# Forty of the sixty-four tile transposes of a decoder layer moved from TensorE to the DMA queue of SyncE

## The chip, the cores and the metric

The kernel runs on the 8 cores of one Trainium2 chip. Each core takes one of the 8 sequences of the batch and computes the whole layer for it; the cores exchange nothing. The metric is device time in microseconds of the slowest core: 1814.36 us as the median of 3 runs of the kernel before (1813.77 to 1814.71). The profile is that of the slowest core, core 4, in one execution.

A core has five engines that run side by side, each through its own list of instructions in order: TensorE (PE) multiplies, ScalarE (ACT) and VectorE (DVE) do the element-wise work and empty the PSUM banks that TensorE writes, GpSimd (POOL) does some element-wise work and issues the loads of the weights, SyncE (SP) issues the other transfers. They wait for one another through semaphores.

## The reference

The layer works on x, 2048 rows of 1024 columns in float32 per core:

```
x = x + 0.5 * swiglu(rmsnorm(x, ffn1_norm), w1, w3, w2)          # first FFN, 2816 wide
h = rmsnorm(x, mix_norm)
u = h @ w_in                                                      # q, k, v, gate, lru x, lru gate
y_ret = (silu(g_ret) * groupnorm(retention(rotary(q), rotary(k), v))) @ w_ret_o
y_lru = (rg_lru(conv(x_lru)) * gelu(g_lru)) @ w_lru_o
g = sigmoid(h @ w_branch_gate + b_branch_gate)
x = x + (g[:, :D] * y_ret + g[:, D:] * y_lru) @ w_out
x = x + softmax(q(rmsnorm(x, xattn_norm)) k(rmsnorm(mem)).T / 16) v @ w_xo   # 256 memory rows, 4 heads
x = x + 0.5 * swiglu(rmsnorm(x, ffn2_norm), ...)                  # second FFN
out = rmsnorm(x, final_norm)
```

So x is normalised five times, and four of the five results (all but the last) are the input of a matrix product.

## The kernel before, in words

x lies in SBUF as 16 tiles X of 128 rows x 1024 columns (tile tt holds rows 128 tt to 128 tt + 127). Four tiles make a row block of 512 rows, called tb. A matmul needs the normalised x with its columns on the partitions, so each tile is turned: hT holds, for each row block, eight pieces of 128 columns by 512 rows in bf16.

`norm_T` does this for one tile. `rstd_of` sums the squares on ScalarE (JUNK), scales on VectorE (stat) and takes the power -0.5 on GpSimd; VectorE writes the normalised tile in bf16 to HB, one of four buffers used in turn (line 936); then the tile is turned. With a PSUM bank given, eight matmuls with the identity write it to that bank (line 948), and ScalarE and VectorE in turn copy the bank into hT (lines 749 and 956). With `bk` None, a transposing transfer on SyncE's queue goes from HB straight to hT:

```
        if bk is None:
            P.add("sp", lambda e: e.dma_start_transpose(out=dst_ap, in_=hb.ap),
                  reads=hb.hs, writes=dst_hs, cost=400, dma=128 * D * 4)
            return
```

`norm_x(tt, row, bk)` calls it for tile tt, four times per tile: at the start (before the first FFN), in `post1` (after the first FFN, for the mixers), in `tail` (after the mixers' output product, for attention) and after attention (for the second FFN). In the three later places a number decides which of the two ways a tile goes:

```
norm_x(tt, mixrow[0], None if tt < TR1 else bkT)     # post1
norm_x(tt, row, None if tt >= TR2 else bkT)          # tail
norm_x(tt, rowf, None if tt < TR3 else bkT)          # after attention
```

In the kernel before, no tile goes by DMA. The handles that track who reads and writes hT cover two tiles each (`hhs(tb, j // 2)`), so the second tile of a pair is a later writer of the same handles as the first.

The stages follow one another: the first FFN in weight groups of 6, 6, 5 and 5 pieces, with the preparation of the memory and of tables in its gaps; the mixers (16 steps of the recurrent unit, 16 blocks of retention, 16 pieces of the gate product GW, whose results go to HBM); `tail`; attention (`scores`, then `outp` per tile); the second FFN; the last norm and the stores. During the mixers x gives up its place: `park` stores each tile to HBM after the first FFN, and `tail` loads it back. `ret_load` loads the weights RW of the retention, `load` in `lru_stages` those of the recurrent unit, LW.

The order of each engine's instructions is not written out by hand. The program first records all operations with their dependencies, an assumed cost and, for transfers, a byte count. `schedule` then plays them through: each engine takes the operation that can start first, and of several the one with the longest path behind it; transfers go by the latest start that a former pass found for them. A throttle (`dma_gate`) lets a queue issue a transfer only when those still in flight count less than `DMA_LIMIT`, 1.1 MB, and adds the wait for the transfer that must have landed. A change in the operations therefore changes the order of everything behind it.

Of the kernel before, what the change touches and what calls it, by code (L numbers as in the profile page):

```python
# [568 lines left out]
GKEEP = 1  # L569
NSPLIT = 2  # L570
RWU = 2
TR1 = 0
TR2 = 16
TR3 = 0
G0 = [0, 1]
G1 = [2, 3]
SIDEG = 1
# [47 lines left out]
def record(stage, plan):  # L625
# [158 lines left out]
    def load_row(name, slot, after=()):  # L784
        v = ROW.v(slot * D, D)
        r = ROWIDX[name]
        sp_dma(v.ap, bass.AP(rows_d.tensor, r * D, [[0, 128], [1, D]]), list(after), v.hs, 128 * D * 4)
        return v
# [169 lines left out]
    def norm_x(tt, row, bk):  # L958
        tb, j = divmod(tt, 4)
        d = hT_tb(tb)  # L960
        norm_T(xt(tt), row, tt, d.ap[:, :, j * 128:(j + 1) * 128], hhs(tb, j // 2), bk)
# [542 lines left out]
    def tail():  # L1504
# [51 lines left out]
        for tt in range(16):  # L1556
# [14 lines left out]
            if stage >= 3:  # L1571
                norm_x(tt, row, None if tt >= TR2 else bkT)

# [81 lines left out]
    def park(tt):  # L1655
        v = xt(tt)
        sp_dma(park_d[tt * 128:(tt + 1) * 128, :], v.ap, v.hs, [h_park[tt]], 128 * D * 4)

    def post1(tt):
        if mixrow[0] is None:  # L1660
            mixrow[0] = load_row("mix_norm", 0)
        if stage >= 2:
            norm_x(tt, mixrow[0], None if tt < TR1 else bkT)
            park(tt)
# [38 lines left out]
    if stage >= 3:  # L1703
        f2 = FFN(1)
        rowf = load_row("ffn2_norm", 1)
        xattn((lambda tt: norm_x(tt, rowf, None if tt < TR3 else bkT)) if stage >= 4 else (lambda tt: None),
              (lambda n: f2.pump(n)) if stage >= 4 else (lambda n: None))
# [73 lines left out]
```

How the kernel before makes its waits and increments, by code:

```python
            def run(ename, eng):  # L441
                waited = {}
                for op in order[ename]:
                    ws = {}
                    for d in waits[op.id]:
                        if d.dma:
                            s, v = dsem[d.eng][d.idx % NDMASEM], 16 * (d.idx // NDMASEM + 1)
                        else:
                            s, v = esem[d.eng], d.semval
                        if waited.get(id(s), 0) >= v:
                            continue
                        waited[id(s)] = v
                        ws[id(s)] = (s, v)
                    for (s, v) in ws.values():
                        eng.wait_ge(s, v)
                    if op.fn is None:
                        continue
                    ins = op.fn(eng)
                    if op.dma:
                        ins.then_inc(dsem[ename][op.idx % NDMASEM], 16)
                    elif op.marked:
                        ins.then_inc(esem[ename], 1)
```

The softmax here doesn't subtract the row's maximum and nothing guards it: scores larger than these inputs give would overflow.

## Time and profile before

| what | us |
|---|---|
| median of 3 runs (lowest, highest) | 1814.36 (1813.77, 1814.71) |
| the profiled execution's own time | 1814.36 |
| its span, slowest core (of 1798.6 to 1812.8) | 1812.8 |
| TensorE busy | 1728.3 (95%) |
| VectorE busy | 884.7 (49%) |
| ScalarE busy | 667.1 (37%) |
| GpSimd busy | 381.1 (21%) |
| DMA queues of GpSimd and SyncE, share of 16 engines | 22.2% and 12.7% |

The span runs from the first to the last instruction of the core; the time has 1.6 us around it. A busy TensorE counts from a matmul's start to its modelled end, and matmuls overlap, so the distance between two starts is shorter than a matmul's duration. The granted clock of TensorE is 0.984 of full speed as a mean over this core.

### The profile page before, as it was taken

How to read it: one execution, taken by the hardware profiler on the slowest of the kernel's cores; microseconds unless marked ns; L12 is line 12 of the kernel's file. 1: busy time of each engine (PE TensorE's matmuls, PEld its weight loads, DVE VectorE, ACT ScalarE, POOL GpSimd, SP SyncE). 2: the span in 40 equal slices, each digit the busy share in tenths (PEclk: the TensorE clock that was granted, in tenths of full speed). 3: DMA queues.
4: the chain of work that ended last, by engine and by line, in shares of the span. 5: the costliest groups of instructions: out<-in, count | busy, mean ns of one | idle time of the engine just before them, and what ended most of it. 6: DMA issues, size and time to landing. Idle time of an engine off the chain costs nothing.

```text
span 1812.8 us, 24773 instructions; the slowest of 8 cores (1798.6 to 1812.8 us)
## 1 busy us (share of the span) xinstructions
PE 1728.3 (95%) x8664; PEld 820.8 (45%) x8664; DVE 884.7 (49%) x1309; ACT 667.1 (37%) x1020; POOL 381.1 (21%) x424
## 2 busy tenths in 40 slices
PE   6999999999998989988999989999999999999997
PEld 4444454444453444434444534444454444444443
DVE  4766523244466666446666433355463332233455
ACT  5411111111246667755676633245441101111122
POOL 2200011100124444342544534211010000000000
PEclk9999999999999999989999999999999999999999
DMA  9844466721451452221211574332040320420022
GB/s 243 153 79 124 106 100 106 132 51 33 126 139 36 90 96 60 52 37 36 49 24 24 129 213 123 105 111 59 1 71 12 48 46 1 70 36 12 6 93 93
DMA packets 56409, 141.63 MB, mean 78 GB/s; under 512 B 5984, under 2 KB 18272, under 8 KB 54240
## 3 DMA queue, kind: packets, MB, share of 16 engines
q0 software_dynamic: 25488, 62.40, 22.2%
q1 hardware_dynamic: 30800, 77.65, 12.7%
q8 instruction: 72, 1.18, 0.3%
q14 instruction: 49, 0.40, 0.1%
HBM read 168.87 MB, written 33.55 MB: 112 GB/s over the span
## 4 chain that ended last, share of the span: by engine, by line
PE 80%; DMA 7%; DVE 5%; issue 4%; ACT 2%; POOL 1%; DVEq 0%; POOLq 0%; ACTq 0%; SPq 0%
PE bank L733 77%; PE bank L948 1%; DMA W<-f_w 1%; DMA WVS<-w_v 1%; DMA rope<-RT 1%; DMA wv_centred<-WVB 1%; DMA XW<-w_xqT 1%; DVE XC L1245 1%; DMA XW<-w_xv 1%; DVE WVB L880 1%; DMA XW<-w_xo 0%; PE bank L1412 0%; DVE T L1323 0%; DVE T L1321 0%; DMA TW<-w_tail 0%
## 5 line engine op out<-in xcount | busy, mean ns | idle before, releaser
L733 PE MATMUL bank<-hT,W 128*128 128x512 bf16 (+1 forms) x2880 | 621.6, 376 | 3.9 <-DVE hT L956 2.2
L733 PEld LDWEIGHTS bank<-hT,W 128*128 128x128 bf16 x2880 | 282.0, 98 | 329.6 <-issue 6.7
L749 ACT ACTIVATE STMP<-bank 128x512 f32<-128x512 f32 x176 | 104.8, 596 | 622.5 <-PE bank L733 603.9
L733 PE MATMUL bank<-W,HID 128*128 128x512 bf16 x1408 | 313.1, 381 | 3.7 <-DVE WVM L878 2.0
L1049 DVE SCALAR_TENSOR_TENSOR X<-bank,X 128x512 f32<-128x512 f32 x256 | 174.8, 689 | 195.3 <-PE bank L733 194.3
L1031 DVE TENSOR_TENSOR HID<-bank,STMP 128x512 bf16<-128x512 f32 x176 | 119.5, 689 | 264.3 <-PE bank L733 263.1
L733 PEld LDWEIGHTS bank<-W,HID 128*128 128x128 bf16 x1408 | 137.5, 98 | 169.8 <-issue 7.4
L762 POOL DMA_DIRECT2D W<-f_w x89 | 48.2, 543 | 532.6 <-PE bank L733 456.4
L749 ACT ACTIVATE JUNK<-X 128x1024 bf16<-128x1024 f32 x80 | 84.4, 1056 | 129.9 <-DVE X L1049 65.4
L928 POOL TENSOR_TENSOR stat<-stat,cst 128x1 f32<-128x1 f32 x82 | 51.9, 634 | 362.4 <-DVE stat L927 362.1
L733 PE MATMUL bank<-hT,RW 128*128 128x512 bf16 x512 | 120.3, 389 | 8.0 <-ACT RS L749 3.5
L733 PE MATMUL bank<-hT,GW 128*128 128x512 bf16 x512 | 115.9, 379 | 0.7 <-DVE GU L1487 0.5
L733 PE MATMUL bank<-hT,LW 128*128 128x512 bf16 x512 | 114.3, 379 | 0.2 <-ACT TR L749 0.2
L936 DVE SCALAR_TENSOR_TENSOR HB<-X,stat,ROW 128x1024 bf16<-128x1024 f32 x64 | 80.9, 1279 | 27.3 <-POOL stat L928 22.9
L1245 DVE SCALAR_TENSOR_TENSOR XC<-XL,pc,XC 128x1024 f32<-128x1024 f32 x48 | 65.0, 1354 | 58.6 <-ACT XL L749 57.2
L1543 DVE SCALAR_TENSOR_TENSOR TT<-TT,bank 128x512 f32<-128x512 f32 x64 | 43.8, 687 | 90.4 <-PE bank L733 83.9
L733 PEld LDWEIGHTS bank<-hT,RW 128*128 128x128 bf16 x512 | 49.9, 100 | 69.6 <-issue 15.7
L733 PEld LDWEIGHTS bank<-hT,LW 128*128 128x128 bf16 x512 | 49.9, 98 | 60.3 <-issue 0.6
L733 PEld LDWEIGHTS bank<-hT,GW 128*128 128x128 bf16 x512 | 49.5, 98 | 59.6 <-issue 1.8
L733 PE MATMUL bank<-ATP,TW 128*128 128x512 bf16 x256 | 61.9, 386 | 7.0 <-DMA TW<-w_tail 7.0
L749 ACT ACT_TABLE_LOAD x48 | 61.6, 1283 | 16.6 <-DMA GIN<-gate_scr 6.2
L749 ACT ACTIVATE TT<-GIN,dcol 128x512 f32<-128x512 f16 x64 | 42.6, 714 | 63.0 <-POOL MG L1547 62.8
(162 smaller groups left out, 1876.2 us busy)
## 6 DMA issues: line engine op xcount, KB each, us to landing
W<-f_w POOLq DMA_DIRECT2D x43, 512.0 KB, 5.9
W<-f_w POOLq DMA_DIRECT2D x46, 256.0 KB, 5.0
X<-x SPq DMA_DIRECT2D x16, 512.0 KB, 9.2
park<-X SPq DMA_DIRECT2D x16, 512.0 KB, 2.7
gate_scr<-GU SPq DMA_DIRECT2D x64, 128.0 KB, 2.2
GIN<-gate_scr SPq DMA_DIRECT2D x8, 1024.0 KB, 7.1
X<-park SPq DMA_DIRECT2D x16, 512.0 KB, 6.8
out<-OST SPq DMA_DIRECT2D x16, 512.0 KB, 2.6
```

What stands on the lines that cost most here:

```text
L733: ins = e.matmul(out_ap, l, r, start=(start and i == 0), stop=(stop and i == n - 1), skip_group_check=skip)
L749: P.add("act", lambda e: e.activation(out, in_, func, **kw), reads=reads, writes=writes, cost=act_cost(n, nap), tab=tab)
L762: P.add("pool", lambda e: e.dma_start(out=out, in_=in_), reads=reads, writes=writes, cost=600, dma=nbytes)
L880: dve(lambda e: e.tensor_tensor(o.ap, w.ap, mb, ALU.subtract), w.hs + m.hs, o.hs, KC * 256)
L928: pool(lambda e: e.tensor_tensor(s[:, 2:3], s[:, 1:2], cc(2), ALU.pow), hs + cst.hs, hs, 550)
L936: dve(lambda e: e.scalar_tensor_tensor(hb.ap, src.ap, r, row.ap, ALU.mult, ALU.mult), src.hs + rh + row.hs, hb.hs, D)
L948: ins = e.transpose(bv[:, c * 128:(c + 1) * 128], hb.ap[:, c * 128:(c + 1) * 128], identb.ap)
L1031: dve(lambda e: e.tensor_tensor(hd.ap, banks[b3][:, :], s.ap, ALU.mult), [hbk[b3]] + s.hs, hd.hs, TB)
L1049: dve(lambda e, b=b, xv=xv: e.scalar_tensor_tensor(xv.ap, banks[b][:, :], 0.5, xv.ap, ALU.mult, ALU.add), [hbk[b]] + xv.hs, xv.hs, 512)
L1245: dve(lambda e, s=s: e.scalar_tensor_tensor(xc.ap, XL.v(s, 1024).ap, pcol("conv_w", s * 8 + c), xc.ap, ALU.mult, ALU.add), xl_all.hs + xc. ...
L1543: dve(lambda e, t=t, by=by: e.scalar_tensor_tensor(t.ap, t.ap, 1.0, banks[by][:, :], ALU.add, ALU.mult), t.hs + [hbk[by]], t.hs, TB)
```

## The change

Three numbers change:

```
-TR1 = 0
-TR2 = 16
-TR3 = 0
+TR1 = 16
+TR2 = 8
+TR3 = 16
```

All 16 tiles after the first FFN, tiles 8 to 15 after the mixers and all 16 tiles after attention are now turned by transfers on SyncE's queue; 24 tiles (16 at the start, 8 after the mixers) and the two tiles of the memory stay on TensorE. The plan is made anew with these operations.

The first place is SyncE's queue between the first FFN and the mixers. Before, the stores of x stand there, and one load of retention weights:

```order
L759 DMA m_scr<-MT 128x2048 x4
L759 DMA v_scr<-MT 128x2048 x4
L759 DMA CS<-rope 128x512 x2
L759 DMA park<-X 128x1024 x5
L759 DMA RW_79<-wv_centred 128x4096
L759 DMA park<-X 128x1024 x11
L759 DMA CS<-rope 128x512 x2
```

Now, with what each waits for (s_dve is VectorE's semaphore; d_sp with a number is the landing of an earlier transfer of this queue, numbered modulo 24, and d_sp1 is the first transpose, d_sp3 the second, d_sp6 the third, d_sp10 the fifth):

```order
L759 DMA park<-X 128x1024 [waits s_dve]
L940 DMA_TRANSPOSE hT<-HB_51 128x8x128 [waits s_dve,d_sp21]
L759 DMA park<-X 128x1024 [waits s_dve,d_sp23]
L940 DMA_TRANSPOSE hT<-HB_52 128x8x128 [waits s_dve,d_sp1]
L759 DMA park<-X 128x1024 [waits s_dve]
L759 DMA park<-X 128x1024 [waits s_dve,d_sp2]
L940 DMA_TRANSPOSE hT<-HB_49 128x8x128 [waits s_dve,d_sp3]
L759 DMA park<-X 128x1024 [waits s_dve,d_sp4]
L759 DMA RW_79<-wv_centred 128x4096 [waits d_sp5,s_dve]
L940 DMA_TRANSPOSE hT<-HB_50 128x8x128 [waits d_sp7,d_sp6]
L940 DMA_TRANSPOSE hT<-HB_51 128x8x128 [waits d_sp8,s_dve]
```

The sixteen transposes stand between the stores, and most wait for the one before to have landed.

The second place is TensorE at the same hand-over: the last products of the first FFN (W_46 with HID), the first of the recurrent unit (hT with LW, XCB with LW) and of the retention (hT with RW_79). Before:

```order
L733 MATMUL bank<-W_46,HID 128x512 x10
L733 MATMUL bank<-hT,LW 128x512 x8
L733 MATMUL bank<-W_46,HID 128x512 x10
L733 MATMUL bank<-hT,LW 128x512 x8
L733 MATMUL bank<-W_46,HID 128x512 x20
L948 MATMUL bank<-identb,HB_51 128x128 x8
L948 MATMUL bank<-identb,HB_52 128x128 x8
L948 MATMUL bank<-identb,HB_49 128x128 x8
L948 MATMUL bank<-identb,HB_50 128x128 x8
L733 MATMUL bank<-hT,RW_79 128x512 x8
L948 MATMUL bank<-identb,HB_51 128x128 x8
L733 MATMUL bank<-hT,RW_79 128x512 x24
```

Now:

```order
L733 MATMUL bank<-W_46,HID 128x512 x10
L733 MATMUL bank<-hT,W_45 128x512 x48
L733 MATMUL bank<-W_46,HID 128x512 x50
L733 MATMUL bank<-hT,LW 128x512 x16
L733 MATMUL bank<-W_46,HID 128x512 x10
L733 MATMUL bank<-hT,RW_79 128x512 x48
L733 MATMUL bank<-XCB,LW 128x512 x4
L733 MATMUL bank<-hT,LW 128x512 x32
L733 MATMUL bank<-hT,RW_79 128x512 x8
```

The transposes are gone, and 48 matmuls of the retention's first three row blocks now stand between the last product of the first FFN and the rows that read the last tiles. In LW x32 the first two groups of eight read the first half of x, the third and fourth the third and the fourth row block.

The third place is TensorE at the end of attention (VP with PX is its output product, W_45 the second FFN's first weights). Before:

```order
L733 MATMUL bank<-VP,PX 128x512 x40
L948 MATMUL bank<-identb,HB_51 128x128 x8
L733 MATMUL bank<-VP,PX 128x512 x16
L948 MATMUL bank<-identb,HB_52 128x128 x8
L948 MATMUL bank<-identb,HB_49 128x128 x8
L948 MATMUL bank<-identb,HB_50 128x128 x8
L733 MATMUL bank<-VP,PX 128x512 x16
L948 MATMUL bank<-identb,HB_51 128x128 x8
L733 MATMUL bank<-VP,PX 128x512 x16
L948 MATMUL bank<-identb,HB_52 128x128 x8
L948 MATMUL bank<-identb,HB_49 128x128 x8
L948 MATMUL bank<-identb,HB_50 128x128 x8
```

Now:

```order
L733 MATMUL bank<-VP,PX 128x512 x24
L733 MATMUL bank<-PEX,onesb 128x512 x2
L733 MATMUL bank<-hT,MS 128x512 x16
L733 MATMUL bank<-VP,PX 128x512 x8
L733 MATMUL bank<-PEX,onesb 128x512 x2
L733 MATMUL bank<-VP,PX 128x512 x88
L733 MATMUL bank<-hT,W_45 128x512 x240
L733 MATMUL bank<-W_46,HID 128x512 x96
```

The output product runs through without a break, and the second FFN begins behind it.

## Rows read from the trace of the kernel before

**Rows 1.** The page's head and its busy times, with shares and instruction counts.

```profile
span 1812.8 us, 24773 instructions; the slowest of 8 cores (1798.6 to 1812.8 us)
PE 1728.3 (95%) x8664; PEld 820.8 (45%) x8664; DVE 884.7 (49%) x1309; ACT 667.1 (37%) x1020; POOL 381.1 (21%) x424
```

**Rows 2.** Stretches: start:end, length, busy us per engine, PE clock, DMA share, GB/s.

```profile
500.00:580.00 80.00, 72.31 (x414) 35.41 (x413) 56.01 (x74) 40.79 (x60) 27.03 (x24) 0.96 0.35 88
580.00:1080.00 500.00, 467.11 (x2356) 223.49 (x2355) 283.27 (x362) 321.82 (x462) 211.36 (x164) 0.97 0.32 71
...
1140.00:1240.00 100.00, 96.72 (x505) 45.90 (x503) 54.32 (x82) 40.34 (x65) 21.50 (x29) 0.97 0.46 119
1240.00:1420.00 180.00, 180.00 (x952) 86.18 (x951) 84.14 (x117) 63.22 (x102) 13.70 (x25) 1.00 0.13 24
1420.00:1780.00 360.00, 360.00 (x1669) 162.82 (x1668) 131.11 (x194) 53.84 (x91) 19.22 (x36) 1.00 0.21 42
```

**Rows 3.** Groups of instructions: count, busy us, mean ns, idle before and releasers.

```profile
L948 PE MATMUL bank<-identb,HB 128*128 128x128 bf16 x528 | 36.9, 223 | 20.0 <-DVE HB L936 17.0 <-DVE hT L956 1.4 <-DVE X L1569 1.3
...
L749 ACT ACTIVATE hT<-bank 128x1024 bf16<-128x1024 bf16 x32 | 32.3, 1021 | 26.6 <-PE bank L948 26.6
...
L956 DVE COPY hT<-bank 128x1024 bf16<-128x1024 bf16 x32 | 21.2, 684 | 6.4 <-PE bank L948 4.2 <-ACT hT L749 2.2
```

**Rows 4.** Timeline of TensorE, end of attention: start, us, instructions, idle before.

```profile
1330.66 1.50 PE L948 MATMUL bank<-identb,HB 128*128 128x128 bf16 x24
1332.00 3.62 PE L733 MATMUL bank<-VP,PX 128*128 128x512 bf16 x16
```

**Rows 5.** Timeline of TensorE, first FFN to mixers.

```profile
506.84 1.89 PE L733 MATMUL bank<-hT,W 128*128 128x512 bf16 x8
...
532.87 4.48 PE L733 MATMUL bank<-W,HID 128*128 128x512 bf16 x20
...
548.84 0.60 PE L948 MATMUL bank<-identb,HB 128*128 128x128 bf16 x8 [1.37 <-DVE hT L956]
...
569.80 0.59 PE L733 MATMUL bank<-XCB,LW 128*128 128x512 bf16 x2 [4.40 <-POOL XCB L1248]
```

**Rows 6.** DMA issues of SyncE: count, KB each, median us to landing.

```profile
CS<-rope SPq DMA_DIRECT2D x16, 256.0 KB, 3.5
...
rope<-RT SPq DMA_DIRECT2D x8, 256.0 KB, 4.6
wv_centred<-WVB SPq DMA_DIRECT2D x4, 512.0 KB, 9.4
```

**Rows 7.** Tile CS: the landing times of its 16 loads.

```profile
DMA to landing us min/median/max: 3.0/3.5/7.6
```

**Rows 8.** Tile WVB: the landing times of its 4 stores.

```profile
DMA to landing us min/median/max: 3.8/9.4/13.8
```

**Rows 9.** Timeline of VectorE: first tile and last tile of the first hand-over.

```profile
447.98 0.69 DVE L1049 SCALAR_TENSOR_TENSOR X<-bank,X 128x512 f32<-128x512 f32 x1 [0.39 <-PE bank L733]
...
451.35 1.28 DVE L936 SCALAR_TENSOR_TENSOR HB<-X,stat,ROW 128x1024 bf16<-128x1024 f32 x1 [0.82 <-POOL stat L928]
...
546.74 1.28 DVE L936 SCALAR_TENSOR_TENSOR HB<-X,stat,ROW 128x1024 bf16<-128x1024 f32 x1
```

**Rows 10.** Tile park: issue times of the stores.

```profile
L759 SPq DMA_DIRECT2D park<-X x16: 319/319/320, 448.7 to 538.5; - x16
```

**Rows 11.** Waits of TensorE for landings: us, times, longest.

```profile
PE bank L733 <- DMA TW<-w_tail: 7.0, 1, 7.0
...
PE bank L733 <- DMA XW<-w_xqT: 2.7, 2, 2.0
...
PE bank L733 <- DMA XW<-w_xo: 1.3, 1, 1.3
PE bank L733 <- DMA XW<-w_xv: 1.1, 2, 0.7
...
PE bank L733 <- DMA W<-f_w: 0.7, 1, 0.7
```

## The prediction

> **What bounds the kernel now.** I read the page's busy times first, then a table of stretches, the rows of the instructions that the change removes, the waits of TensorE, and last the timeline around the three places where the normalised x changes its layout. TensorE is busy for 1728.3 of 1812.8 us [rows 1], so only its own work, and the 84.5 us in which it stands, can shorten the span. The table of stretches shows where it stands [rows 2]: 7.7 us where the first FFN hands over to the mixers (500 to 580), 32.9 us inside the mixers (580 to 1080), 3.3 us where the mixers hand over to attention (1140 to 1240), and nothing at all from 1240 to 1780, attention and the second FFN. So whatever work leaves TensorE after 1240 comes off the time in full, as long as nothing new arrives late there; in the mixers other engines share the bound, and a saving may be eaten.
>
> **What goes.** Sixty-six tiles are turned on TensorE (64 of x, 2 of the memory), eight 128x128 matmuls each, x528, and the results are copied out of PSUM by ScalarE (1021 ns) and VectorE (684 ns) in turn [rows 3]. The change takes 40 of the 66, 320 matmuls: the 16 of the first hand-over, 8 of the second, 16 of the third (attention to the second FFN). What one costs TensorE is the distance between starts, since the next matmul begins before the last one's modelled end: three tiles begin at 1330.66 and the next work at 1332.00, so 1.34 / 3 = 0.447 us a tile [rows 4]. 40 x 0.447 = 17.9 us. The busy time gives the upper end: 36.9 us / 66 = 0.56 us, 22.4 us for 40. I take 17.9, the distance, because that is what the following matmul feels. One of the waits goes too: at 548.84 TensorE stood 1.37 us for VectorE's copy before the last transposes of the first hand-over [rows 5]; 0 to 1.4, I take 1.4. The 20 copies of ScalarE (20 x 1.021 = 20.4 us) and 20 of VectorE (13.7 us) lie beside TensorE's work and are priced at nothing; what hides them is that both engines are busy for about half of the span or less [rows 1].
>
> **What comes: forty transfers on SyncE's queue.** The trace has no transposing transfer, so its time from issue to landing, L, is bounded by rows. A tile is 128 x 1024 x 2 B = 256 KB. Plain transfers of 256 KB on the same queue land after 3.5 us (CS, at best 3.0) and 4.6 us (rope, out of SBUF) [rows 6, 7]. The slow end is the transfer that is cut most: wv_centred writes 1024 pieces of 512 B and takes 9.4 us, at worst 13.8 [rows 6, 8]; a transposed tile is 128 partitions x 8 pieces, 1024 pieces too. So L lies between 3.0 and 13.8. I take 4.6, the row with the same bytes, source and queue; both ends stay for the range.
>
> The Trainium skill speaks on both sides here. Its page "Advanced Engine Details and Errata", section "X-Bar Transpose (TRN2)", says that transposing transfers run as fast as ordinary ones, which is the 4.6 us. Its page "VectorE: DVE Perf Modes", section "The three transpose paths", gives a 128x128 block 390 ns on TensorE and 1309 ns by DMA; TensorE's row above has 0.447 / 8 = 0.056 us, so the first figure does not hold in a dense stream, and the second, taken eight times one after another, would be an estimated 10.5 us a tile. No run here shows it yet. By the first rule the sum below stands. By the second the chain of twelve (below) would be 12 x 10.5 - 97.4 = 28.6 us late and the time about 1824 us; that is the rival that ends slower, and it is priced there from rows alone.
>
> **First hand-over.** Here the transfers are nearly a chain. The second tile of each pair waits for its partner (they share handles of hT), and the throttle, which counts a transpose as 512 KB, makes most first tiles wait for the pair before: tiles 0, 1, 2, 3, 5, 6, 8, 9, 10, 11, 14, 15 follow one another, 12 links. The first can start when its HB is written, 451.35 + 1.28 = 452.6 [rows 9]. When must the last have landed? TensorE's order is the same as before up to the weights that start at 506.84 [rows 5]; from there the changed order has 48 + 50 + 16 + 10 + 48 + 4 + 24 = 200 matmuls up to the first that reads the last four tiles (the fourth group of eight in LW x32). A matmul takes 360.00 / 1669 = 0.2157 us [rows 2], so that point is 506.84 + 43.1 = 550.0. The chain has 97.4 us for 12 L and is in time up to L = 8.1. x itself keeps the pace: its tiles are parked from 448.7 to 538.5, one in 6.0 us [rows 10]. The second limit is the last tile alone: its last matmul ends at 506.84 + 124 x 0.2157 = 533.6, and from there to a written HB the trace has 4.7 us where VectorE is free (447.98 to 452.6) and 10.7 us where it is crowded (532.87 + 4.48 = 537.35 to 546.74 + 1.28 = 548.02) [rows 5, 9]. The crowded value leaves 5.7 us for L, just above 4.6. So lateness = the larger of 12 L - 97.4 and L - 5.7: nothing at 4.6, 15.4 us at 9.4, 68 us at 13.8. Queued behind a waiting transfer on SyncE stand the next park stores and one RW load; nobody reads those for tens of microseconds.
>
> **Second and third hand-over.** Tiles 8 to 15 of the second are turned only after the last load of x has been issued. Between the last PE transpose, whose HB buffer tile 11 needs, and the first score matmul of the third row block the changed order has 124 matmuls, 26.7 us; they must hold three HB writes (3.8 us) and two transfers, so L up to 11.4 is free, and 13.8 costs 4.7. In the third, TensorE's row with x240 begins with 6 weight tiles x 2 row blocks x 2 products x 8 = 192 matmuls on the first two blocks, 41.4 us, before it touches the tiles of the third block; from the first tile to the need of the last there are some 590 matmuls, 127 us, for two chains of 8 links each, so even 13.8 (110 us) is in time. VectorE may stand for one of the four HB buffers there, but a buffer comes back after two transfers at the most. I price both at nothing beyond the next term.
>
> **Small waits.** A hand-over by DMA is not free in this kernel: leaving out TW, TensorE waited 2.7 + 1.3 + 1.1 + 0.7 = 5.8 us in six waits for landings that were planned in time, 1.0 us each [rows 11]. Three hand-overs, 3.0 us; bounds 0 and, at the 7.0 us of TW, 21. From the first hand-over to the end of the mixers the planner orders all engines anew; that can take away or add a wait of the size that stretch has (7.0 at the most), so 0, plus or minus 7.
>
> **Sum.** -17.9 - 1.4 + 3.0 = -16.3 us. The profiled execution itself took 1814.36 us (1812.8 span and 1.6 around it), which is the median of the three runs, so the forecast is 1798 us. Its own range is 1790 (22.4 + 1.4 saved, no wait) to 1805.
>
> **Rivals.** *The first share is eaten (1806 us).* In the mixers TensorE stands 32.9 of 500 us; if their start is paced by VectorE's and ScalarE's chain, the 7.2 + 1.4 us saved at the first hand-over come back as waits, such as the 4.40 us that stand at 569.80 now [rows 5]. Left are 24 x 0.447 = 10.7 less 2 x 1.0, so 1814.4 - 8.7. For it: that wait has nothing to do with a transpose. Against: TensorE is at 93% there.
>
> *The chain of twelve is late (slower).* If a transfer takes more than 9.7 us, 12 L - 97.4 exceeds the 19.3 us saved, and the first hand-over costs more than all three save: 1814.4 - 19.3 + 68 + 5 = 1868 at 13.8. For it: the only row with as many pieces has 9.4. Against: its pieces go to HBM beside a 1 MB load, and it once landed in 3.8 [rows 8]. Loads of LW, RW and GW share the engines in this stretch and push L up.
>
> *No change (about 1812).* Two new waits of 7 us in the reordered mixers. *More than forecast (below 1787).* The new order closes a good part of the 32.9 us by chance.
>
> **Chances.** Forecast 0.56, first share eaten 0.15, late chain 0.18, no change 0.07, more 0.04. A measurement of this kernel tells 0.2%, 3.6 us, from no change: faster 0.56 + 0.15 + 0.04 = 0.75, same 0.07, slower 0.18. The range 1787 to 1820 holds the first two, the fourth, half of the last and the near end of the late chain, 0.83.
>
> **What would show it.** TensorE's rows with identb and HB fall from x528 to x208 and some 22 us less of busy time; 40 transposing transfers land in about 4.6 us; TensorE has no wait over 3 us between 527 and 555, and none from 1240 to 1780, where the stretch is shorter by 7 us. L above 8, or a wait of TensorE for hT at the first LW matmuls, makes the chain the story. A shorter third stretch together with an unchanged end of the mixers makes it the eaten share. If TensorE loses the matmuls and the span does not follow, the step "distance between starts" is wrong.

## The result and the profile after

The changed kernel takes 1787.57 us (median of 4 runs, 1785.82 to 1795.1), the kernel before 1814.07 (4 runs): a ratio of 0.9865 with a 95% interval of 0.9834 to 0.9895, 26.5 us less, where 16.3 less were forecast. The profiled execution took 1789.07 us, 1787.4 of them the span of core 1. Executions in which one die ran at a visibly lower granted clock are left out of every time below.

The head of the page after, beside [rows 1], and then the groups of the transposes that are left, beside [rows 3]:

```profile
span 1787.4 us, 24179 instructions; the slowest of 8 cores (1769.0 to 1787.4 us)
PE 1707.4 (96%) x8344; PEld 804.7 (45%) x8344; DVE 876.6 (49%) x1289; ACT 648.9 (36%) x1002; POOL 374.1 (21%) x424
```

```profile
L948 PE MATMUL bank<-identb,HB 128*128 128x128 bf16 x208 | 16.8, 236 | 17.8 <-DVE HB L936 14.5 <-DVE stat L927 1.9 <-DVE X L1569 1.3
L749 ACT ACTIVATE hT<-bank 128x1024 bf16<-128x1024 bf16 x12 | 12.2, 1021 | 19.7 <-PE bank L948 19.7
L956 DVE COPY hT<-bank 128x1024 bf16<-128x1024 bf16 x12 | 8.2, 687 | 4.4 <-PE bank L948 4.0 <-ACT hT L749 0.3
```

320 matmuls and 40 copies are gone, and 20.9 us of TensorE's busy time. Its table of stretches, beside [rows 2] (same columns):

```profile
500.00:580.00 80.00, 75.61 (x354) 33.96 (x352) 56.39 (x73) 42.36 (x63) 26.36 (x24) 1.00 0.52 111
580.00:1080.00 500.00, 474.31 (x2391) 227.67 (x2389) 284.30 (x363) 322.75 (x467) 214.48 (x171) 0.98 0.34 76
1140.00:1240.00 100.00, 86.69 (x423) 39.83 (x422) 51.92 (x74) 39.83 (x67) 14.35 (x22) 0.91 0.64 125
1240.00:1420.00 180.00, 180.00 (x836) 81.59 (x835) 76.44 (x106) 51.02 (x87) 15.32 (x28) 1.00 0.31 54
```

TensorE stands 4.4 us instead of 7.7 at the first hand-over and 25.7 instead of 32.9 in the mixers, but 13.3 instead of 3.3 at the second hand-over, where its clock also fell (0.91).

Stretches of fixed times hold different work in the two kernels. The table below cuts every core's trace at the same matmuls instead: the start of the first FFN's last 48 matmuls with hT and W, its last matmul with W and HID, the last with TW (end of the mixers), the first and the last with VP and PX (attention), the last of the second FFN with W and HID. Each value is the median of the 8 cores, us; in brackets the time in which TensorE stood.

| stage | before | after | transposes gone x 0.447 |
|---|---|---|---|
| first FFN up to there (same work) | 504.7 | 501.7 | 0 |
| its end | 30.1 | 26.5 | 3.6 (8 tiles) |
| mixers | 622.3 (40.9) | 603.6 (30.3) | 3.6 (8) |
| second hand-over | 76.9 (2.6) | 72.1 (3.4) | 3.6 (8) |
| attention | 98.7 (0.0) | 101.8 (2.8) | 2.2 (5) |
| second FFN | 461.9 (1.0) | 457.4 (1.4) | 4.9 (11) |

The end of the first FFN and the second FFN give what the matmuls were worth. The second hand-over and attention together give 1.7 us of 5.8. The mixers give 18.7 us for 3.6: more than half of the whole gain. The first 500 us, the same work, came out 3 us shorter for no reason that lies in the change.

The time goes by the slowest core and not by medians: the medians' sum falls by 31.5 us, the span by 25.4. In the profiled execution the three slowest cores (1, 3 and 7, 1783.5 to 1787.4 us) took 180.8 to 185.4 us for the second hand-over and attention together, the other five 170.0 to 172.9; before, the eight took 173.4 to 178.8. So these two stages became shorter on five cores and longer on the three that set the time.

What the transfers do on SyncE's queue (instruction time min/median/max in ns, start of the first and the last, then issue to landing):

```profile
L940 SPq DMA_TRANSPOSE hT<-HB x40: 1217/1222/6182, 447.5 to 1329.0; - x40
...
  DVE HB L936: 13.4, 2
...
DMA to landing us min/median/max: 3.0/3.2/19.6
```

Half of them land within 3.2 us, the worst after 19.6, and VectorE waited 13.4 us for them in two waits. By stretch, the same rows give a median of 5.1 us for the sixteen of the first hand-over, 6.8 for the eight of the second, 3.1 for the last fourteen of the third.

First hand-over on TensorE, beside [rows 5]:

```profile
501.61 10.52 PE L733 MATMUL bank<-hT,W 128*128 128x512 bf16 x48
511.97 10.96 PE L733 MATMUL bank<-W,HID 128*128 128x512 bf16 x50
522.76 3.62 PE L733 MATMUL bank<-hT,LW 128*128 128x512 bf16 x16
526.21 2.32 PE L733 MATMUL bank<-W,HID 128*128 128x512 bf16 x10
528.37 10.52 PE L733 MATMUL bank<-hT,RW 128*128 128x512 bf16 x48
538.73 0.59 PE L733 MATMUL bank<-XCB,LW 128*128 128x512 bf16 x2
539.80 0.38 PE L733 MATMUL bank<-XCB,LW 128*128 128x512 bf16 x1 [0.47 <-DVE T L1323]
540.52 0.38 PE L733 MATMUL bank<-XCB,LW 128*128 128x512 bf16 x1 [0.34 <-DVE SG L1336]
540.73 7.07 PE L733 MATMUL bank<-hT,LW 128*128 128x512 bf16 x32
```

No row waits for hT: the chain of twelve is in time. The last of the sixteen transposes was issued at 536.59 and landed after 5.5 us; the last eight matmuls of LW x32, which read it, begin some 4 us later, at about 545.9.

Second hand-over, the second wait of VectorE for a buffer, ScalarE behind it, TensorE behind both:

```profile
1222.92 1.28 DVE L936 SCALAR_TENSOR_TENSOR HB<-X,stat,ROW 128x1024 bf16<-128x1024 f32 x1 [10.37 <-DMA hT<-HB]
```

```profile
1227.23 1.06 ACT L749 ACTIVATE JUNK<-X 128x1024 bf16<-128x1024 f32 x1 [10.42 <-DVE X L1619]
...
1228.81 1.26 ACT L749 ACTIVATE PEX<-bank 128x512 bf16<-128x512 f32 x2
```

```profile
1215.95 3.62 PE L733 MATMUL bank<-hT,MS 128*128 128x512 bf16 x16
1219.40 1.89 PE L733 MATMUL bank<-VP,PX 128*128 128x512 bf16 x8
1230.21 1.01 PE L733 MATMUL bank<-PEX,onesb 128*128 128x512 bf16 x2 [8.92 <-ACT PEX L749]
1231.02 6.11 PE L733 MATMUL bank<-hT,MS 128*128 128x512 bf16 x16
1236.97 1.89 PE L733 MATMUL bank<-VP,PX 128*128 128x512 bf16 x8
1238.70 0.59 PE L733 MATMUL bank<-PEX,onesb 128*128 128x512 bf16 x2
1239.13 3.62 PE L733 MATMUL bank<-hT,MS 128*128 128x512 bf16 x16
```

A transfer holds an HB buffer, VectorE stands 10.37 us before it can write the next tile, ScalarE stands 10.42 us for the X that VectorE owes, so the exponentials PEX come late and TensorE stands 8.92 us. After that the same sixteen matmuls take 6.11 us instead of 3.62, another 2.5 us: the granted clock (the third number from the end) had fallen to a mean of 0.57, near the lower of TensorE's two levels (1.2 and 2.4 GHz).

```profile
1230.00:1237.00 7.00, 6.79 (x19) 2.47 (x20) 3.25 (x4) 1.89 (x4) 0.00 (x0) 0.57 0.34 65
```

The issues between 1180 and 1230 (KB each, median us to landing) show what stands beside the transposes there:

```profile
W<-f_w POOLq DMA_DIRECT2D x4, 512.0 KB, 11.5
ROW<-rows SPq DMA_DIRECT2D x1, 512.0 KB, 4.3
hT<-HB SPq DMA_TRANSPOSE x8, 6.8
```

### The profile page after: what moved, and what is told of

It reads as the page before. It is cut to its first block, busy times and chain, and to the rows that moved or that the text cites. A ratio compares the mean times of both kernels' runs of the same rounds, so it can differ in the third digit from the quotient of the medians.

```text
span 1787.4 us, 24179 instructions; the slowest of 8 cores (1769.0 to 1787.4 us)
## 1 busy us (share of the span) xinstructions
PE 1707.4 (96%) x8344; PEld 804.7 (45%) x8344; DVE 876.6 (49%) x1289; ACT 648.9 (36%) x1002; POOL 374.1 (21%) x424
## 2 busy tenths in 40 slices
DMA packets 98647, 152.09 MB, mean 85 GB/s; under 512 B 48224, under 2 KB 60512, under 8 KB 96480
## 4 chain that ended last, share of the span: by engine, by line
PE 84%; DMA 6%; issue 3%; DVE 3%; ACT 2%; POOL 1%; DVEq 0%; POOLq 0%; ACTq 0%; SPq 0%
PE bank L733 81%; DMA W<-f_w 2%; DMA hT<-HB 1%; DMA XW<-w_xv 1%; DMA XW<-w_xqT 1%; DVE XC L1245 1%; PE bank L948 1%; DVE T L1323 0%; POOL MU L1279 0%; POOL QK L1326 0%; DMA X<-x 0%; ACT L749 0%; DMA XW<-w_xo 0%; DMA out<-OST 0%; DVE XC L1285 0%
## 5 line engine op out<-in xcount | busy, mean ns | idle before, releaser
L749 ACT ACTIVATE JUNK<-X 128x1024 bf16<-128x1024 f32 x80 | 84.5, 1056 | 141.7 <-DVE X L1049 63.2
```

Source lines behind the costliest of these rows:

```text
L749: P.add("act", lambda e: e.activation(out, in_, func, **kw), reads=reads, writes=writes, cost=act_cost(n, nap), tab=tab)
```

## The experiments

Each is compared with runs of the kernel before that were taken beside it on the same chip: a median of 1815.67 us for e1 to e4, 1818.06 for e5, e6, e8 and e9, and 1825.05 for e7, e10, e11 and e12. Stage times come from one profiled execution each, as medians of its 8 cores.

**One share at a time.** Two theories: the mixers' gain belongs to the first hand-over ("new plan"), or is spread; and the second share is eaten by crowded transfers.

```
 e1    TR1, TR2, TR3 = 16, 16, 0      (first hand-over alone)
 e2    TR1, TR2, TR3 = 0, 8, 0        (second alone)
 e3    TR1, TR2, TR3 = 0, 16, 16      (third alone)
 e4    TR1, TR2, TR3 = 16, 16, 16     (all but the second)
```

> Only the first hand-over (first FFN to mixers) is turned by DMA; the second and third stay on TensorE. Theory 'new plan': most of the gain comes from the mixers, which this hand-over orders anew (TensorE's waits between the end of the first FFN and the last TW matmul fall from about 41 to 30 us per core, the stretch from 622 to 604 us), so this kernel alone gains about 3.6 + 18.7 = 22 us, about 1791 us. Rival 'forty equal savings': each of the 16 tiles is worth its 0.45 us of TensorE, 7 us, about 1807 us.

> Only tiles 8 to 15 of the second hand-over (mixers to attention) are turned by DMA. Theory 'crowded transfers': the transposes that meet the loads of the second FFN's weights land after 9 to 20 us in place of 3, VectorE stands for a free HB buffer and TensorE behind it, so the 3.6 us of matmuls saved are lost again: no change to 6 us slower, 1813 to 1820 us, with a TensorE wait of 2 to 9 us in attention's first row block. Rival 'saved in full': 3.6 us faster, about 1810 us.

> Only the third hand-over (attention to the second FFN) is turned by DMA. Both theories: 16 x 0.447 = 7.2 us faster, about 1807 us, since TensorE has no gap there and the cover is tens of microseconds; mixers unchanged at about 622 us per core. Rival 'handed-over late': less than 4 us faster, with a wait of TensorE at the start of the second FFN.

> First and third hand-over by DMA, the second all on TensorE. Theory 'crowded transfers': the wait of 2 to 9 us of TensorE in attention's first row block goes, 3.6 us of transposes come back: the slowest cores gain most, so 0 to 5 us faster than the changed kernel, 1783 to 1788 us. Rival 'saved in full' (the eight transfers of the second hand-over pay): 3.6 us slower than the changed kernel, about 1791 us.

| kernel | us | ratio | end of first FFN | mixers | second hand-over | attention | second FFN |
|---|---|---|---|---|---|---|---|
| e1 | 1792.98 | 0.9880 (0.9848 to 0.9911) | 26.5 | 604.7 | 78.0 | 99.0 | 462.0 |
| e2 | 1816.95 | 1.0011 (0.9991 to 1.0031) | 30.1 | 622.3 | 71.5 | 105.8 | 461.9 |
| e3 | 1807.43 | 0.9977 (0.9938 to 1.0016) | 30.1 | 622.7 | 77.3 | 96.4 | 457.0 |
| e4 | 1783.66 | 0.9835 (0.9809 to 0.9860) | 26.5 | 603.3 | 79.3 | 96.7 | 457.0 |

The four times came as the first-named theory of each expectation had them. The first share alone comes with the shorter mixers, 604.7 us, with nothing else changed; whether by its transfers or by the order that the planner made with them is asked below. The third brings 4.9 us in the second FFN and 2.3 in attention, 7.2 in all, which is 16 x 0.447; its time agrees (8.2 us less) but shows it less surely: two of its eight executions took 1826 us, and the interval reaches past 1. The second alone is worth nothing: attention is 7.1 us longer, the hand-over 5.4 shorter. Between e4, which leaves it out, and the full change the runs don't decide: the intervals of the ratios overlap (0.9835 and 0.9865), and second hand-over and attention take 176.0 us in e4 against 173.9. Why the hand-over of e4 is 2.4 us longer than before, with the same transposes in it, stays open.

In e2 VectorE waits for the transfers and TensorE behind it, as in the full change:

```profile
  DVE HB L936: 8.9, 3
...
DMA to landing us min/median/max: 3.0/6.2/13.8
```

```profile
1251.45 1.01 PE L733 MATMUL bank<-PEX,onesb 128*128 128x512 bf16 x2 [4.53 <-ACT PEX L749]
```

**Keep the weights away from the transposes of the second hand-over.** The first weights of the second FFN are loaded only after the last of those transposes: the loads are given the last row block of hT, `hhs(3)`, to wait for (a second line, not shown, passes the argument on). TensorE's rows stand in the same order in both traces; a few of VectorE's and ScalarE's move.

```
-        pump(5)
+        pump(5, hhs(3))
```

> The changed kernel, but the loads of the second FFN's first weights wait until the last transposes of the second hand-over have landed; TensorE's order is the same. Theory 'crowded transfers': the eight transposes land after 3 to 5 us in place of 3 to 20, VectorE's wait for HB (13.4 us on the profiled core) and TensorE's wait behind it (0.3 to 8.9 us by core) go, and the time is 3 to 9 us below the changed kernel, 1779 to 1785 us, also below the kernel with only the first and third hand-over (1783.7) by up to 3.6. Rival 'the transposes slow themselves' (pairs in flight together): landing times stay near 10 us and the time at 1787.

1777.99 us (1777.01 to 1781.68), ratio 0.9775 (0.9757 to 0.9794). In the trace of its core 7, all transposes, then the eight of the second hand-over alone (issued from 1185 to 1222), and what TensorE still waits for from 1140 to 1325:

```profile
L940 SPq DMA_TRANSPOSE hT<-HB x40: 1217/1222/2376, 451.0 to 1323.5; - x40
...
DMA to landing us min/median/max: 3.0/3.2/9.6
```

```profile
L940 SPq DMA_TRANSPOSE hT<-HB x8: 1217/1220/2376, 1186.6 to 1216.4; - x8
...
DMA to landing us min/median/max: 3.0/3.2/5.2
```

```profile
PE bank L733 <- ACT PEX L749: 0.9, 1, 0.9
PE bank L733 <- DVE X L1569: 0.8, 1, 0.8
PE bank L948 <- DVE HB L936: 0.4, 1, 0.4
```

The eight land after 3.0 to 5.2 us, as expected; the 9.6 belongs to the end of the third hand-over, beside the next 512 KB weight loads. The wait of 8.9 us is gone (no core stands longer than 0.9 us in this stretch, where the change had up to 8.9), VectorE has none for a transfer, the longest SyncE instruction falls from 6.2 to 2.4 us. Second hand-over and attention take 69.9 + 98.6 = 168.5 us: 5.4 less than in the change and 7.1 less than before. Pairs of transposes are in flight together here too, and land after 3.1 to 3.3 us, so the rival falls: the loads beside them, not the transposes themselves, had eaten that share. The time is 1 us below the expected range.

**Another plan of the same work.** If the mixers owe their gain to the transposes, a change of a number in the planner should leave 622 and 604 us as they are. e6 lowers the assumed cost of a transpose on TensorE in the kernel before; e8 and e9 set the assumed hold of an activation table to 700 ns in before and after; e10 and e12 set it to 500; e7 sets the assumed cost of a semaphore to 75 ns in the kernel after. None changes an operation of the layer, only the order, and with it how often ScalarE loads an activation table (46 to 50 times, 1.283 us each).

```
 e6            -cost=8 * 64     +cost=8 * 56          (before)
 e8, e9        -TAB_HOLD = 600  +TAB_HOLD = 700       (before, after)
 e10, e12      -TAB_HOLD = 600  +TAB_HOLD = 500       (before, after)
 e7            -SEM_NS = 70     +SEM_NS = 75          (after)
```

> The kernel before with one assumed cost of the planner changed (a tile's transposes 448 in place of 512 ns), all tiles on TensorE. Theory 'new plan by the hand-over': the mixers' stretch stays at 618 to 626 us per core. Rival 'luck of the plan': it moves by 5 us or more, since any change of a number gives another order.

> The kernel before with another assumed number changed (the planner's reluctance to change ScalarE's table 700 in place of 600 ns); all tiles on TensorE. Theory 'new plan by the hand-over': mixers 618 to 626 us per core. Rival 'luck of the plan': mixers move by 5 us or more, perhaps to the 604 us of the changed kernel, without a single transfer more.

> The changed kernel with the same number changed (700 in place of 600 ns); 40 tiles by DMA as there. Theory 'new plan by the hand-over': mixers stay at 600 to 608 us per core. Rival 'luck of the plan': they move by 5 us or more.

> The kernel before, no transfer added, with the planner's assumed hold of an activation table at 500 ns instead of 600 (700 gave 1797 us and mixers of 605.6 us, against 622.3). Theory A, the mixers of before are long because their start is tied to the transposes of the first hand-over, and 700 was a rare exception: mixers again 620 to 625 us and a time of 1812 to 1820. Theory B, the mixers' length is what one plan of many happens to have, and the plan of before is a poor one: mixers at another value, anywhere from 603 to 630 us, with the 7 us wait for TW gone or a new one in its place, and a time that follows, 1795 to 1825. A time within 4 us of 1816 with the same three waits (TW, RS, T) speaks for A.

> The changed kernel with that same number at 500 ns. With 600 its mixers took 603.6 us, with 700 they took 595.2. Theory A (the transposes by transfer are what shortens the mixers): 595 to 606 us again, time 1776 to 1790. Theory B (luck of the plan, of either sign): another value, and it may as well lie above 606 us, up to 618, with a time up to 1803. At an equal number the changed kernel should stay below the kernel before by at least the 3.6 us of the eight tiles whose transposes left the mixers, under both theories.

> The changed kernel with the planner's assumed cost of a semaphore at 75 ns instead of 70, another plan of the same work. Theory A: mixers 595 to 606 us, time 1776 to 1790. Theory B: any value up to 618 us, time up to 1803. The second FFN and the attention don't depend on it: 457 us, and 101 to 105 with crowded transfers at the second hand-over (up to 10 us of wait on a core).

One execution each, but for before and after; the third column is the kernel before, measured beside it. "TensorE stood" is its idle time in the mixers; "slow matmuls" adds up by how much neighbouring starts in a row without a wait lie further apart than 0.2157 us; both are medians of the cores.

| kernel | us | before, beside it | mixers | TensorE stood | slow matmuls | mixers less both |
|---|---|---|---|---|---|---|
| before | 1814.07 | | 622.3 | 40.9 | 7.5 | 573.9 |
| e6, before, transpose cost | 1818.43 | 1818.06 | 623.3 | 40.2 | 9.4 | 573.7 |
| e8, before, 700 | 1797.33 | 1818.06 | 605.6 | 27.0 | 6.3 | 572.3 |
| e10, before, 500 | 1845.99 | 1825.05 | 641.6 | 56.1 | 17.6 | 567.9 |
| after | 1787.57 | 1814.07 | 603.6 | 30.3 | 4.8 | 568.5 |
| e9, after, 700 | 1776.52 | 1818.06 | 595.2 | 23.4 | 5.3 | 566.5 |
| e12, after, 500 | 1830.86 | 1825.05 | 644.5 | 52.6 | 21.2 | 570.7 |
| e7, after, semaphore | 1813.59 | 1825.05 | 625.5 | 42.4 | 15.2 | 567.9 |

Of the expectations, e6's theory held (623.3; TensorE's order hardly changed there). e8 and e9 moved by 16.7 and 8.4 us, as the rival said. e10, e12 and e7 left the ranges of both theories, in the mixers and in the time, all to the slow side; only the second FFN (457.0) and attention (104.1) of e7 came as expected.

The mixers of the kernel before lie between 606 and 642 us, those of the change between 595 and 645, with the same operations in another order. At an equal hold the change's are shorter by 18.7 (600 ns) and 10.4 (700), and longer by 2.9 (500). The fewest table loads (46, e7 and e12) go with long mixers and the most (50, after) with short ones, so these loads are not the reason. Less the standing and the slow matmuls, the four of before average 572.0 us and the four of after 568.4. The difference of 3.6 is what the eight transposes that left would give, but the values of one kernel lie up to 6 us apart, so it agrees with them and does not prove it. A length like that of the change (605.6) is had without one transfer, so the 15 us beyond the transposes need no transfer; that they are the order's luck is the plain reading. Whether the change makes a good order likelier, three pairs don't tell. In time the change is the faster at each hold, by 26.5, 20.8 (700) and 15.1 us (500); of the last, which compares two single executions, the sums of the stage medians show nothing (1811.8 and 1812.1 us), since the slowest core of e10 lies 18 us above the median of its cores.

The waits of TensorE in the mixers (us, times, longest), of the kernel before, of e10, of e8 and of the kernel after, each on its slowest core, show what an order does. In e8 and after, there is no wait for the weights TW at all:

```profile
PE bank L733 <- DMA TW<-w_tail: 7.0, 1, 7.0
PE bank L733 <- ACT RS L749: 5.2, 4, 2.7
PE bank L733 <- DVE T L1323: 5.0, 4, 2.4
```

```profile
PE bank L733 <- DMA TW<-w_tail: 12.9, 1, 12.9
PE bank L733 <- DVE T L1323: 9.6, 6, 2.4
PE bank L733 <- ACT RS L749: 6.8, 3, 3.3
```

```profile
PE bank L733 <- POOL XCB L1248: 4.7, 2, 4.3
PE bank L1412 <- DVE SC L1375: 3.7, 3, 2.5
PE bank L1434 <- DVE T L1323: 2.8, 1, 2.8
```

```profile
PE bank L1434 <- DVE T L1323: 2.8, 1, 2.8
PE bank L733 <- POOL ATP L1458: 2.7, 1, 2.7
PE bank L1412 <- DVE SC L1375: 2.7, 2, 2.2
```

Theory A of the last three expectations falls: the mixers of the kernel before are not tied to its transposes, and those of the change are not held short by its transfers. Whether 700 is better than 500 by a rule (it was in both kernels) or by chance, two points each don't tell.

**Both edits that helped.** e11 has the held weights of e5 and the hold of 700 ns of e9.

> The changed kernel with both edits that helped: the second FFN's first weights wait for the last transposes of the second hand-over (alone 1778.0 us), and the hold at 700 ns (alone 1776.5, one run). If the two gains lie in different stages they add: mixers 595 us as with 700 alone, second hand-over and attention 169 us as with the held weights alone (175.7 with 700 alone), so 1768 us, 1764 to 1773. Rival: the later start of the weight loads gives time back in the second FFN (a wait for W at its start), and the time stays at 1775 to 1779.

1776.27 us (1772.66 to 1779.37) beside 1825.05 for the kernel before: 0.9736 (0.9708 to 0.9764), the lowest ratio. Its mixers take 597.5 us, second hand-over and attention 69.8 + 99.0 = 168.8, the second FFN 457.4. In the stages the two gains add, nearly as expected, and the wait for W that the rival named is not there. The time, 1776.27 us, misses the expected 1764 to 1773 and lies in the rival's range, but the kernel before ran 7 us slower here than beside e5 and e9, from which the expectation started. As ratios to it the expected 1768 us is 0.972, inside the interval, and the rival's 1775 to 1779 is 0.976 to 0.979, at its edge. The interval overlaps that of e5 (0.9757 to 0.9794), so by how much e11 beats e5 is not settled.

## Why the prediction was right, and where it was not

The direction came by the mechanism, the closeness in part by luck. 1787.57 us lies 2.4 us under the forecast's own range (1790 to 1805) and 0.6 us inside the wider one (1787 to 1820); two of the four executions lie below both. Two terms that the sum had at nothing went opposite ways: the order of the mixers gave some 15 us, and the second hand-over took back 4.1 us by the medians and some 12 between the slowest cores (178.8 us before, 185.4 after, where 5.8 should have left).

*TensorE bounds the span, so matmuls that leave it come off in full: right where nothing new arrives late.* From 1240 to 1420 TensorE still does not stand (180.00 of 180.00), in the second FFN it stands 1.4 us against 1.0, and the third share came in full (e3: 7.2 us for 16 x 0.447 = 7.2). The distance between starts, not the modelled duration, was the price: 0.56 us a tile would have given 9.0 there. The end of the first FFN fell by 3.6 for eight tiles.

*L = 4.6, and the chain of twelve is in time: right in its result.* With little else in flight a transposing transfer landed in 3.0 us, the lower bound, so CS and not rope was its row; in the crowded first hand-over the median was 5.1 and the longest 7.1, under the limit of 8.1, and the last tile's 5.5 was just under its own limit of 5.7. No row waits for hT, so the chain of twelve being late is refuted. The count of pieces, for which wv_centred's 9.4 us was the slow end, did not set L: packets under 512 B rose from 5984 to 48224, 1056 for each transpose, and L was still 3.0. By the Trainium skill's page "Advanced Engine Details and Errata", section "X-Bar Transpose (TRN2)", transposing transfers are as fast as ordinary ones; the trace agrees for the fastest of either, with 3.0 us beside CS's 3.0 [rows 7]. The 1309 ns per block on the Trainium skill's page "VectorE: DVE Perf Modes", section "The three transpose paths", would be an estimated 10.5 us for eight blocks one after another; the trace shows 3.0 at best and 3.2 in the median for a tile of eight.

*The second hand-over at nothing: wrong.* The step that failed is "they must hold three HB writes (3.8 us) and two transfers, so L up to 11.4 is free, and 13.8 costs 4.7". One L was used for all places, and the loads of the second FFN's weights, which GpSimd's queue starts just there, were not counted. With them L reached 19.6. The path was wrong too: the step follows a tile to its own score matmuls, but the wait came by way of two engines that work in order, VectorE standing for the HB buffer and ScalarE behind it for X, which held up the exponentials of scores that TensorE had finished by 1219.6 (the x16 before the wait). The 5.8 us of thirteen tiles shrank to 1.7 (median of the cores; core 1 paid 8.92 and 2.5 more). e5 undoes this by moving those loads alone. The small waits of 3.0 us, thought of as 1.0 at each hand-over, came as nothing at the first and third and some 4 at the second.

*Re-ordering at 0, plus or minus 7: mis-sized, and the largest part of why the time was missed by 10.4 us.* The mixers fell by 15 us beyond their transposes. I bounded the term by the longest single wait of the stretch, but a new order adds and removes many waits together, and with more standing came a lower clock (a mean of 0.95 over 580 to 1080 in e10, 0.99 in e8): from e10 to e8 the same operations differ by 36 us. Another 3 us by the medians, 5 between the slowest cores, come from the first 500 us, where no cause is shown. "More than forecast", the rival in which the new order closes a good part of the 32.9 us by chance, is what happened there (to 25.7 in the same stretch), and it had been given 0.04. The forecast's sum without this term (-16.3) is near the change's own worth; that worth alone, 3.6 + 3.6 + 1.7 + 4.5 = 13.4 us by stages, is smaller than the spread of the orders. That the time became faster rests on a good order as much as on the transposes: with 500 ns the same change measured 1830.86 us, beside 1825.05 for the kernel before at its own 600 ns and 1845.99 for it at 500.

*The first share is eaten: not borne out.* In e1 the end of the first FFN gave its 3.6 us whole, and the mixers were 17.6 us shorter; how much of their own 3.6 is in that, apart from the order, no run tells. *No change* came only in the stage medians of e12 beside e10, under another setting of the planner.

## What to carry to other kernels

Where a planner orders everything anew, measure a change under several of its settings, in the kernel before as well, and read the gain from the stages that hold the changed work; the spread of the orders here was larger than the gain. Price a new transfer at each place by what else is issued in the same microseconds, and ask which buffer it holds, which engine stands for that buffer, and what else stands behind that engine. A load that could as well start later may then be worth more than the transfer itself.

## What the runs showed of the hardware

- A transposing transfer of a 128 x 1024 bf16 tile, out of SBUF into SBUF, landed in 3.0 us where little else was in flight, and took SyncE 1.22 us to issue, against 0.32 us for a store of x [rows 10].
- Beside 512 KB weight loads on GpSimd's queue the same transfer landed after up to 19.6 us and SyncE's issue took up to 6.18 us; with the loads held back (e5), 5.2 and 2.38 in the same hand-over. The loads themselves landed after 11.5 us there (median of four).
- A transposing transfer of such a tile goes in 1056 packets under 512 B (5984 before, 48224 with forty of them).
- A wait of 8.92 us cost TensorE another 2.5 us behind it: sixteen matmuls took 6.11 instead of 3.62 us at a granted clock of 0.57. In the mixers slow matmuls cost 5 us in the order with the least standing (23.4 us, e9) and 18 to 21 in the two with the most (56.1 and 52.6, e10 and e12).
